# Hybrid decoder trunk, two layers on one core: another order of the attention stage around the projections

## The chip, the cores and the metric

One NeuronCore of a Trainium2 chip runs the whole program. The metric is the device time in microseconds (us) from start to end of one execution. TensorE (PE) multiplies, VectorE (DVE), ScalarE (ACT) and GpSimd (POOL) do the elementwise work, SyncE's queue (SP) issues the loads. Each engine works through its own list of instructions in order and waits on semaphores.

## The reference

256 tokens, width 1024, two layers. Per layer:

```python
h = rms_norm(x, attn_norm)
qa, ka, va, qd, kd, vd = split(h @ w_in)          # 6 groups of 512 columns, 8 heads of 64 each
out_a = rms_norm(causal_attention(rope(qa), rope(ka), va), moba_out_norm)
out_d = rms_norm(dilated_attention(rope(qd), rope(kd), vd), dil_out_norm)
x = x + concat(out_a, out_d) @ w_out
x = x + square(relu(rms_norm(x, mlp_norm) @ w_up)) @ w_down
```

and at the end `rms_norm(x, final_norm)`. With 256 tokens and blocks of 256 the block-sparse attention is plain causal attention. The dilated attention mixes three patterns of window and stride, each weighted by its softmax denominator; this is one softmax over the scores plus the logarithm of how many patterns hold the key.

## The kernel before

**Precision by splitting.** Every weight and every left operand exists as a high part (a cast) and a low part (the rest). ScalarE casts a unit of weights from `raw` to `w_hi` (`hi`, L447), VectorE subtracts it into `w_lo` (`lo`, L611), and PE makes three matmuls of 512 columns per product (`three`, L890 to L894). Weights come in chunks of two units; a ring holds four chunks, eight units. A load into a ring slot waits for the splits of the chunk that was there (`load`, L277), a cast waits until PE has used the unit that was in `w_hi` (`weights_used`, L445).

**Steps.** In a layer the input projection has 48 steps s, eight to each of the six groups, in the order dilated q, k, v, causal q, k, v (`GROUP_COLUMNS`). A step of `project_in` (L928) is one eighth of the depth for both token halves: six matmuls, three into the bank of each half; the groups take banks 0, 1 and 2, 3 in turn. Steps 48 to 55 are the output projection for the dilated heads. Then comes the projection for the causal heads, interleaved with steps 56 and 57, and the MLP.

**What hangs on the steps.** After the matmuls of step s, PE does in `attention(l, s)` (L988) what tables at L87 to L104 name for s:

- `ROPE_AT`, `V_AT` (s = 8, 16, ...): VectorE forms the rotation products of a finished q or k group, both token halves (`rope_products`, L656), and GpSimd sums them (`rope_sum`, L377); ScalarE copies a v group (L511).
- `QKT_AT`: PE turns rotated columns into `t_bank` in four transposes (L999), ScalarE copies them to `q_t` or `k_t` (L519). Before: steps 14, 15, 20, 21, 39, 41, 44, 47.
- `QK_PAIRS_AT`: PE makes the scores of a pair of heads, or of two pairs (`score_pair`, L964). Before: one pair at each of 23, 27, 31, 35, two at 46 and at 50.
- `QK_AT`: VectorE masks the scores of a head (L734, L737), ScalarE takes exponentials (L540). One step later, `NORM_AT`: VectorE normalises (`norm`, L635). Three steps later, `PT_AT`: PE turns the probabilities into the same `t_bank` (three transposes, L1008), ScalarE copies them (L526). Before: masks at 23, 25, ..., 37 and 46 to 53, so probability turnings at 26, 28, ..., 40 and 49 to 56.
- `PV_AT`: PE makes the products with v for one or two pairs of heads (L1024, L1027), ScalarE squares them and makes their high parts (L459, L462), VectorE the low parts (L626), GpSimd adds the squares (`add_squares`, L385).
- `STAT_D`: PE sums the squares of the dilated heads over columns (L1041), VectorE forms the mean (`o_mean`).

**The order on each engine is written out.** Within a step, ScalarE does v, the copy of rotated columns, the copy of turned probabilities, the product's squares and high parts, the exponentials, and last a cast (`HI_AT`) (L506 to L551). VectorE does mask, normalisation, rotation products, a split on odd steps only, low parts (L723 to L751). In `attention`, PE does the turning of rotated columns first, then that of probabilities, then products, scores, and the sum of squares. `t_bank` is one bank, so the turning of probabilities waits for every copy of rotated columns asked for up to this step:

```python
pe.wait_ge(p_copied, l * N_HEADS + h + 1)
pe.wait_ge(qk_copied, l * 8 + sum(x_ <= s for x_ in QKT_AT) + 1)
```

Of the kernel before, what the change touches and what calls it, by code (L numbers as in the profile page):

```python
# [37 lines left out]
ACT = mybir.ActivationFunctionType  # L38

P = 128  # L40
# [5 lines left out]
N_HEADS = D_MODEL // HEAD_DIM  # L46
# [9 lines left out]
TOK = SEQ // P  # L56
# [55 lines left out]
def hybrid_kernel(nc, x_d, w_in, w_out, w_up, w_down, final_g, gain_rows_d, ident_d, masks_d, rope_d,  # L112
                  out_d):
    ctx = ExitStack()
    with ctx:
# [3 lines left out]
        def sem(name):  # L119
            return ctx.enter_context(nc.semaphore(name))  # L120
# [72 lines left out]
        split_done = sem("split_done")  # L193
        weights_used = sem("weights_used")
        x_updated = sem("x_updated")
        x_mid = sem("x_mid")
# [47 lines left out]
        def used(l, u):  # L244

            return l * UNITS + u + (1 + UNITS_HELD)

        def turned_tile(x_or_m, k):
# [176 lines left out]
        def _(act):  # L425
# [46 lines left out]
            for l in range(DEPTH):  # L472
# [33 lines left out]
                for s in range(2 * ATT_UNITS):  # L506
                    if s in V_AT:
                        g = V_AT[s]
                        act.wait_ge(weights_used, used(l, 4 * g + 3))
                        act.wait_ge(rstd_done, l * STATS + ST_X + 1)  # L510
                        for t in range(TOK):  # L511
                            last = act.activation(v[:, V_GROUPS[g], t, :], banks[2 * (g % 2) + t][:, :],
                                                  ACT.Copy, scale=rstd[:, ST_X, t:t + 1])
                        last.then_inc(v_done, 1)
                    if s in QKT_AT:
# [88 lines left out]
        def _(dve):  # L604
# [51 lines left out]
            def rope_products(l, g, t):  # L656

                j = ROPE_GROUPS[g]
                dve.wait_ge(weights_used, used(l, 4 * g + 3))
# [4 lines left out]
                bank = banks[2 * (g % 2) + t]  # L664
# [28 lines left out]
            for l in range(DEPTH):  # L693
# [29 lines left out]
                for s in range(2 * ATT_UNITS):  # L723
                    u = s // 2 + LO_AHEAD
                    if s == STAT_D + 1:
                        o_mean(l, ST_D, stat_d)
                    if s in QK_AT:
# [4 lines left out]
                                 (exp_done, l * N_HEADS + h + 1))  # L732
                        bank = early_banks.get(h, s_banks[h % 2])
                        dve.tensor_tensor_reduce(out=scores[:, h % 2, 0:P], in0=bank[:, 0:P], in1=m[:, P:2 * P],  # L734
# [7 lines left out]
                    if s in ROPE_AT:  # L742
                        if ROPE_GROUPS[ROPE_AT[s]] == 0:
                            scale_rope(l)
                        for t in range(TOK):
                            rope_products(l, ROPE_AT[s], t)
                    if s % 2 == 1 and u < 2 * FIRST_UP + 1:
# [4 lines left out]
                    if s in X_AT:  # L752
# [5 lines left out]
                        add_to_x(acc_d[t][n], t, n, ST_D, x_d_added)  # L758
                o_mean(l, ST_A, stat_a)
                dve.wait_ge(rstd_done, l * STATS + ST_A + 1)  # L760
# [112 lines left out]
        def _(pe):  # L873
# [54 lines left out]
            def project_in(l, s):  # L928
                u = s // 2
                g, k = u // 4, u % 4 * 2 + s % 2  # L930
                c = u // 2
                cols = slice((k % 4) * BANK, (k % 4 + 1) * BANK)
                if l == 0 and s < 6:
                    first_project_in(k)
                    return
                if s == 1:
                    pe.wait_ge(first_lo_half, l)
                elif s % 2 == 0:
                    unit_ready(l, c, u % 2)
                if g == 0:  # L940
                    pe.wait_ge(turned_lo, l * TRS + TR_X + k + 1)
                if k == 0 and g in (2, 3, 5):

                    pe.wait_ge(rope_terms, l * 8 + 2 * ROPE_GROUPS[g - 2] + 2)
                if k == 0 and g == 1 and l == 0:
                    pe.wait_ge(gains_kept, 1)
                if k == 0 and g == 4:
                    pe.wait_ge(v_done, l * 2 + 1)
                for t in range(TOK):
                    tok = slice(t * P, (t + 1) * P)  # L950
                    last = three(banks[2 * (g % 2) + t][:, :], xt[:, k, 0, tok], xt[:, k, 1, tok],
                                 w_hi[:, c % RING, cols], w_lo[:, c % RING, cols], k == 0, k == KT - 1)
                    if t == TOK - 1 and s % 2 == 1:
                        last.then_inc(weights_used, 1)

# [8 lines left out]
            def score_pair(l, h):  # L964
                hh = h % SET_HEADS
                if hh % 4 == 0:

                    pe.wait_ge(qk_copied, l * 8 + 4 * (h // SET_HEADS) + hh // 4 + 4)
                if h == SET_HEADS:
                    pe.wait_ge(rope_terms, l * 8 + 8)  # L970
                elif h == SET_HEADS + 2:
                    pe.wait_ge(mean_done, l * STATS + ST_D + 1)
                elif h == SET_HEADS + 4:
                    pe.wait_ge(v_done, l * 2 + 2)
                elif h == SET_HEADS + 6:
# [3 lines left out]
                outs = [early_banks.get(h + e, s_banks[e]) for e in range(2)]  # L979
                rows = [slice(e * HEAD_DIM, (e + 1) * HEAD_DIM) for e in range(2)]  # L980
# [7 lines left out]
            def attention(l, s):  # L988
# [22 lines left out]
                if s in PV_AT:  # L1011
                    pairs = PV_AT[s]
                    st = pairs[0] // SET_PAIRS
                    pe.wait_ge(p_copied, l * N_HEADS + 2 * pairs[-1] + 3)
                    pe.wait_ge(v_done, l * 2 + st + 1)
# [76 lines left out]
            for l in range(DEPTH):  # L1092
# [56 lines left out]
                project_out(l, acc_a, 7, u0 + 3, 0, 0, False, True).then_inc(acc_a_done, 1)  # L1149
                sum_squares(l, 1, stat_a)  # L1150
                for t, n in ((1, 0), (0, 1)):
# [66 lines left out]
```

## Time and profile before

| what | value |
| --- | --- |
| median of 3 runs | 599.85 us (599.79 to 599.92) |
| the profiled execution | 599.85 us, span 598.1 us |
| busy PE, DVE, ACT, POOL | 589.3, 393.9, 316.8, 46.5 us |
| projection and attention, first layer | about 17 to 120 us of the span |
| the same in the second layer | about 303 to 412 us |
| chain that ended last | 98% PE |

Starts are counted from the start of the span. Matmuls are pipelined: the time that a matmul of a run adds is the distance of its start from the start before it, not its duration. The same holds for short instructions on VectorE and ScalarE.

### The profile page before, as it was taken

Reading aid. Unit: us, or ns where it says so; the run is one execution under the profiler, and the core shown is the slowest. Engines: PE = TensorE matmul, PEld = TensorE weight load, DVE = VectorE, ACT = ScalarE, POOL = GpSimd, SP = SyncE. Lnnn points to the kernel's source line nnn. Section 1 sums busy time; section 2 is a strip of 40 time slices with the busy share of each in tenths; the row PEclk is TensorE's granted clock in tenths of the full one; section 3 lists DMA queues with packets and bytes.
Section 4 is the critical chain, followed back from the end, with each engine's and each line's share of the span. In section 5 each row is a group of like instructions: output and inputs, shape, how many; then the busy total and the mean of one; then the engine's idle time right before and its main releaser. Section 6 shows DMA issues by size and latency. Waiting matters only on the chain.

```text
span 598.1 us, 8728 instructions
## 1 busy us (share of the span) xinstructions
PE 589.3 (99%) x3066; PEld 485.0 (81%) x3066; DVE 393.9 (66%) x655; ACT 316.8 (53%) x536; POOL 46.5 (8%) x51
## 2 busy tenths in 40 slices
PE   8999999999999999999999999999999999999995
PEld 5877777788888888888888777878888888888884
DVE  5866958687755755656388478677875755755634
ACT  5747749475535435344284567674654435435322
POOL 0220230110000000000004013001100000000001
PEclk9999999999999999999999999999999999999999
DMA  8954344248665464564266434431877465465301
GB/s 303 354 212 142 141 141 142 71 140 276 220 222 196 151 236 174 169 250 143 71 209 212 141 140 142 133 112 45 269 249 249 141 219 201 149 224 188 105 0 70
DMA packets 58842, 104.00 MB, mean 174 GB/s; under 512 B 1808, under 2 KB 35264, under 8 KB 58816
## 3 DMA queue, kind: packets, MB, share of 16 engines
q1 hardware_dynamic: 58320, 102.87, 50.7%
q10 hardware_dynamic: 496, 0.81, 0.4%
q8 instruction: 14, 0.23, 0.2%
q14 instruction: 12, 0.10, 0.1%
HBM read 102.62 MB, written 1.05 MB: 173 GB/s over the span
## 4 chain that ended last, share of the span: by engine, by line
PE 98%; DVE 1%; issue 0%; POOLq 0%; POOL 0%; ACT 0%; DVEq 0%; ACTq 0%
PE psum L1051 20%; PE psum L892 20%; PE psum L894 19%; PE psum L893 19%; PE psum L1054 10%; PE psum L1008 2%; PE psum L1024 1%; PE psum L899 1%; PE psum L999 1%; PE psum L985 1%; PE psum L983 1%; PE psum L882 1%; PE psum L1027 1%; PE psum L914 1%; PE psum L920 0%; PE psum L923 0%
## 5 line engine op out<-in xcount | busy, mean ns | idle before, releaser
L611 DVE TENSOR_TENSOR w_lo<-raw,w_hi 128x1024 fp32r<-128x1024 f32 x188 | 229.4, 1256 | 51.4 <-ACT w_hi L447 51.4
L447 ACT CAST w_hi<-raw 128x1024 fp32r<-128x1024 f32 x188 | 187.0, 1049 | 3.0 <-DMA raw<-in_w_in 3.0
L1051 PE MATMUL psum<-xt,w_hi 128*128 128x512 f32 x512 | 160.8, 395 | 0.0
L892 PE MATMUL psum<-w_hi,ot_hi 128*128 128x512 f32 x320 | 127.5, 398 | 0.0
L894 PE MATMUL psum<-w_hi,ot_lo 128*128 128x512 f32 x320 | 125.0, 391 | 0.0
L893 PE MATMUL psum<-w_lo,ot_hi 128*128 128x512 f32 x320 | 124.9, 390 | 0.0
L1054 PEld LDWEIGHTS psum<-xt,w_lo 128*128 128x128 f32 x512 | 96.2, 188 | 22.3
L1054 PE MATMUL psum<-xt,w_lo 128*128 128x256 f32 x512 | 100.8, 278 | 0.0
L1051 PEld LDWEIGHTS psum<-xt,w_hi 128*128 128x128 f32 x512 | 80.3, 189 | 2.3
L558 ACT COPY up_cross<-psum 128x512 f32<-128x512 f32 x32 | 18.8, 588 | 118.8 <-PE psum L1054 118.8
L892 PE MATMUL psum<-w_hi,xt 128*128 128x512 f32 x180 | 74.3, 413 | 0.0
L784 DVE TENSOR_TENSOR up_cross<-psum,up_cross 128x512 f32<-128x512 f32 x32 | 22.1, 692 | 74.0 <-ACT up_cross L558 74.0
L894 PE MATMUL psum<-w_hi,xt 128*128 128x512 f32 x180 | 70.7, 393 | 0.0
L894 PEld LDWEIGHTS psum<-w_hi,ot_lo 128*128 128x128 f32 x320 | 60.1, 188 | 12.9
L893 PE MATMUL psum<-w_lo,xt 128*128 128x512 f32 x180 | 70.4, 391 | 0.0
L892 PEld LDWEIGHTS psum<-w_hi,ot_hi 128*128 128x128 f32 x320 | 60.1, 188 | 12.6 <-issue 2.1
L893 PEld LDWEIGHTS psum<-w_lo,ot_hi 128*128 128x128 f32 x320 | 60.2, 188 | 10.4
L562 ACT CAST ot_hi<-up_sq 128x512 fp32r<-128x512 f32 x32 | 19.9, 622 | 56.3 <-DVE up_sq L787 56.3
L540 ACT ACTIVATE probs<-scores,row_bias 128x128 f32<-128x128 f32 x64 | 28.7, 451 | 25.2 <-DVE row_bias L737 25.2
L892 PEld LDWEIGHTS psum<-w_hi,xt 128*128 128x128 f32 x180 | 33.9, 188 | 9.2 <-issue 3.0
L894 PEld LDWEIGHTS psum<-w_hi,xt 128*128 128x128 f32 x180 | 33.8, 188 | 7.4
L893 PEld LDWEIGHTS psum<-w_lo,xt 128*128 128x128 f32 x180 | 34.0, 189 | 5.7
(85 smaller groups left out, 445.5 us busy)
## 6 DMA issues: line engine op xcount, KB each, us to landing
raw<-in_w_up SPq DMA_DIRECT2D x32, 1024.0 KB, 5.5
raw<-in_w_down SPq DMA_DIRECT2D x32, 1024.0 KB, 6.7
raw<-in_w_in SPq DMA_DIRECT2D x21, 1024.0 KB, 5.5
raw<-in_w_out SPq DMA_DIRECT2D x8, 1024.0 KB, 4.9
raw<-in_w_in SPq DMA_DIRECT2D x3, 512.0 KB, 7.8
raw<-in_w_in SPq DMA_DIRECT2D x4, 256.0 KB, 4.6
out<-x SPq DMA_DIRECT2D x3, 256.0 KB, 2.4
raw<-in_w_in ACTq DMA_DIRECT2D x2, 256.0 KB, 5.1
```

Source lines behind the costliest of these rows:

```text
L447: act.copy(w_hi[:, slot, part], raw[:, slot, part]).then_inc(hi_done, 1)
L540: last = act.activation(probs[:, h % 4, cols], scores[:, h % 2, cols], ACT.Exp, scale=-1.0, bias=row_bias[:, h % 2, t:t + 1], accum_out=ro ...
L558: act.copy(up_cross[:, :, :], up_banks[b][:, :, SEQ:2 * SEQ]).then_inc(cross_copied, 1)
L562: act.copy(h_hi[:, b, :, :], up_sq[:, :, :]).then_inc(h_hi_done, 1)
L611: dve.tensor_tensor(w_lo[:, slot, part], raw[:, slot, part], w_hi[:, slot, part].bitcast(F32), ALU.subtract).then_inc(split_done, 1)
L784: dve.tensor_tensor(up_cross[:, :, :], up_banks[b][:, :, 0:SEQ], up_cross[:, :, :], ALU.add)\
L892: pe.matmul(out, s_hi, m_hi, start=first, stop=False)
L893: pe.matmul(out, s_hi, m_lo, start=False, stop=False)
L894: return pe.matmul(out, s_lo, m_hi, start=False, stop=last)
L1008: last = pe.transpose(t_bank[:, n * P:(n + 1) * P], probs[:, h % 4, n * P:(n + 1) * P], ident[:, :])
L1051: pe.matmul(up_banks[b][:, f, :], w_hi[:, slot, cols[f]], xt[:, k, :, :].rearrange("p a b -> p (a b)"), start=k == 0, stop=False)
L1054: last = pe.matmul(up_banks[b][:, f, SEQ:2 * SEQ], w_lo[:, slot, cols[f]], xt[:, k, 0, :], start=False, stop=k == KT - 1)
```

## The change

Five things. The groups after the first go through banks 2 and 3 alone, and by token half: four steps for the first 128 tokens (all depths), then four for the others, each step six matmuls as before (group 0 keeps its old order, in a function `first_group` that is not shown); a new semaphore `half_done` tells that the first half is there, and rotation products and v copies are taken half by half. The dilated scores come four heads at a time, at steps 22 and 32, in banks 0, 1, 4 and 5. Masks of the dilated heads are at steps 22, 24, 26, 28 and 32, 34, 36, 38, so their probabilities are turned at 25, 27, 29, 31 and 35, 37, 39, 41. Turnings of rotated columns are at 14, 15, 19, 20, 37, 39, 43, 46; causal scores at 45 and 49; products at 32 (two pairs), 42, 52, 56. The sum of squares of the dilated heads goes from step 45 to 47 and from a score bank to the output bank. The order within a step, on every engine, stays.

```diff
-QK_AT = {23 + 2 * h if h < 8 else 38 + h: h for h in range(N_HEADS)}
+QK_AT = {22 + 2 * h if h < 4 else 24 + 2 * h if h < 8 else 37 + h: h for h in range(N_HEADS)}
 NORM_AT = {s + 1: h for s, h in QK_AT.items()}
 PT_AT = {s + 3: h for s, h in QK_AT.items()}
-PV_AT = {31: (0,), 35: (1,), 41: (2, 3), 53: (4, 5), 57: (6, 7)}
-QK_PAIRS_AT = {23: (0,), 27: (2,), 31: (4,), 35: (6,), 46: (8, 10), 50: (12, 14)}
-SQUARES_LATE = {58: (6, 7)}
+PV_AT = {32: (0, 1), 42: (2, 3), 52: (4, 5), 56: (6, 7)}
+QK_PAIRS_AT = {22: (0, 2), 32: (4, 6), 45: (8, 10), 49: (12, 14)}
+SQUARES_LATE = {57: (6, 7)}
 LAST_PAIR = {p: pairs[-1] for pairs in PV_AT.values() for p in pairs}
-QKT_AT = {14: 0, 15: 1, 20: 2, 21: 3, 39: 4, 41: 5, 44: 6, 47: 7}
-ROPE_AT = {8 * g + 8: g for g in ROPE_GROUPS}
-V_AT = {8 * g + 8: g for g in V_GROUPS}
+QKT_AT = {14: 0, 15: 1, 19: 2, 20: 3, 37: 4, 39: 5, 43: 6, 46: 7}
+ROPE_AT = {8: ((0, 0), (0, 1))} | {8 * g + 4 * t + 4: ((g, t),) for g in ROPE_GROUPS if g > 0 for t in range(TOK)}
+V_AT = {8 * g + 4 * t + 4: (g, t) for g in V_GROUPS for t in range(TOK)}
 TAIL = 56
-STAT_D = 45
+STAT_D = 47
...
-V_AT_LAST = max(V_AT)
-HI_AT = {s + int(s == V_AT_LAST): s // 2 + HI_AHEAD for s in range(0, 2 * ATT_UNITS, 2)}
+HI_AT = {s + int(s % 8 == 4 or s in V_AT): s // 2 + HI_AHEAD for s in range(0, 2 * ATT_UNITS, 2)}
...
-        early_banks = {8: banks[0], 9: banks[1], 12: banks[2], 13: banks[3]}
+        more_banks = {h: banks[h % 2] for h in (2, 3, 6, 7, 8, 9)} | {12: banks[2], 13: banks[3]}
...
-        stat_d, stat_a = s_banks[0][:, 3 * P:3 * P + TOK], o_bank[:, 0:TOK]
+        stat = o_bank[:, 0:TOK]
...
+        def group_bank(g, t):
+            return banks[2 * int(g > 0) + t]
...
             def project_in(l, s):
+                g = s // 8
+                if g == 0:
+                    first_group(l, s // 2, s)
+                    return
+                t, j = s % 8 // 4, s % 4
+                u = 4 * g + j
+                if t == 0:
+                    unit_ready(l, u // 2, u % 2)
...
+                if j == 0 and g - 1 in V_GROUPS:
+                    pe.wait_ge(v_done, l * 4 + t + 1)
+                elif j == 0 and g > 1:
+                    pe.wait_ge(rope_terms, l * 8 + 2 * ROPE_GROUPS[g - 1] + t + 1)
+                tok = slice(t * P, (t + 1) * P)
+                for k in (2 * j, 2 * j + 1):
+                    cols = slice((k % 4) * BANK, (k % 4 + 1) * BANK)
+                    last = three(group_bank(g, t)[:, :], xt[:, k, 0, tok], xt[:, k, 1, tok],
+                                 w_hi[:, u // 2 % RING, cols], w_lo[:, u // 2 % RING, cols], k == 0, k == KT - 1)
+                if t == 1:
+                    last.then_inc(weights_used, 1)
+                elif j == 3:
+                    last.then_inc(half_done, 1)
...
-                if h == SET_HEADS:
-                    pe.wait_ge(rope_terms, l * 8 + 8)
-                elif h == SET_HEADS + 2:
-                    pe.wait_ge(mean_done, l * STATS + ST_D + 1)
+                if h == 2:
+                    pe.wait_ge(rope_terms, l * 8 + 2)
                 elif h == SET_HEADS + 4:
-                    pe.wait_ge(v_done, l * 2 + 2)
+                    pe.wait_ge(v_done, l * 4 + 4)
                 elif h == SET_HEADS + 6:
                     pe.wait_ge(masked, l * N_HEADS + SET_HEADS + 4)
-                elif h >= 2:
-                    pe.wait_ge(masked, l * N_HEADS + h)
+                elif h >= 4:
+                    pe.wait_ge(masked, l * N_HEADS + h - 2)
...
+                    if pairs[0] == SET_PAIRS:
+                        pe.wait_ge(mean_done, l * STATS + ST_D + 1)
...
                 if s == STAT_D:
-                    pe.wait_ge(masked, l * N_HEADS + SET_HEADS)
-                    sum_squares(l, 0, stat_d)
+                    pe.wait_ge(o_split, l * PAIRS + SET_PAIRS)
+                    sum_squares(l, 0, stat)
```

## Rows read from the trace of the kernel before

**Rows 1.** The page, busy time and share of the span by engine.

```profile
PE 589.3 (99%) x3066; PEld 485.0 (81%) x3066; DVE 393.9 (66%) x655; ACT 316.8 (53%) x536; POOL 46.5 (8%) x51
```

**Rows 2.** PE's timeline, layer 0, steps 16 to 39: start, us, engine, line, op, count.

```profile
31.62 0.39 PE L893 MATMUL psum<-w_lo,xt 128*128 128x512 f32 x1
...
37.99 0.39 PE L894 MATMUL psum<-w_hi,xt 128*128 128x512 f32 x1
...
38.23 0.60 PE L999 MATMUL psum<-ident,roped 128*128 128x128 f32 x4
...
38.90 0.40 PE L893 MATMUL psum<-w_lo,xt 128*128 128x512 f32 x1
...
73.50 0.60 PE L999 MATMUL psum<-ident,roped 128*128 128x128 f32 x4
```

**Rows 3.** PE's timeline, layer 0, around three score steps.

```profile
43.02 0.39 PE L894 MATMUL psum<-w_hi,xt 128*128 128x512 f32 x1
...
43.33 0.49 PE L983 MATMUL psum<-k_t,q_t 64*128 64x128 f32 x4
...
44.53 0.39 PE L893 MATMUL psum<-w_lo,xt 128*128 128x512 f32 x1
...
57.16 0.40 PE L894 MATMUL psum<-w_hi,xt 128*128 128x512 f32 x1
...
59.48 0.39 PE L893 MATMUL psum<-w_lo,xt 128*128 128x512 f32 x1
...
86.66 0.40 PE L894 MATMUL psum<-w_hi,xt 128*128 128x512 f32 x1
...
88.84 0.40 PE L893 MATMUL psum<-w_lo,xt 128*128 128x512 f32 x1
```

**Rows 4.** PE's and VectorE's timelines, layer 0, first steps of the causal output projection.

```profile
113.14 0.40 PE L894 MATMUL psum<-w_hi,ot_lo 128*128 128x512 f32 x1
...
113.52 0.47 PE L892 MATMUL psum<-w_hi,ot_hi 128*128 128x512 f32 x1
...
112.89 0.88 DVE L626 SCALAR_TENSOR_TENSOR ot_lo<-psum,gains,ot_hi 128x256 fp32r<-128x256 f32 x2 [3.11 <-ACT ot_hi L462]
```

**Rows 5.** ScalarE's timeline, layer 0.

```profile
45.07 0.40 ACT L540 ACTIVATE probs<-scores,row_bias 128x128 f32<-128x128 f32 x1 [2.85 <-DVE row_bias L737]
...
45.97 1.24 ACT L512 ACTIVATE v<-psum,rstd 128x512 f32<-128x512 f32 x2
...
47.11 1.04 ACT L447 CAST w_hi<-raw 128x1024 fp32r<-128x1024 f32 x1
...
74.14 0.59 ACT L519 COPY q_t<-psum 128x512 f32<-128x512 f32 x1 [0.40 <-PE psum L999]
```

**Rows 6.** VectorE's timeline, layer 0.

```profile
31.45 0.68 DVE L671 TENSOR_TENSOR rope_a<-psum,rope_r 128x512 f32<-128x512 f32 x1
...
33.97 3.51 DVE L611 TENSOR_TENSOR w_lo<-raw,w_hi 128x1024 fp32r<-128x1024 f32 x2
...
44.40 0.29 DVE L734 CUSTOM_DVE_ANT_0 scores<-psum,masks 128x128 f32<-128x128 f32 x1 [5.78 <-issue]
...
44.96 1.22 DVE L611 TENSOR_TENSOR w_lo<-raw,w_hi 128x1024 fp32r<-128x1024 f32 x1
...
46.09 0.17 DVE L637 RECIPROCAL row_inv<-row_sum 128x2 f32<-128x2 f32 x1
...
46.76 0.29 DVE L734 CUSTOM_DVE_ANT_0 scores<-psum,masks 128x128 f32<-128x128 f32 x1
```

**Rows 7.** GpSimd: its timeline, and the tile `roped` (ns min/median/max).

```profile
34.13 2.27 POOL L382 TENSOR_TENSOR roped<-rope_a,rope_b 128x512 f32<-128x512 f32 x1
...
67.94 0.74 POOL L394 TENSOR_TENSOR o_sum<-o_sq 128x256 f32<-128x256 f32 x1 [1.87 <-ACT o_sq L459]
...
L382 POOL TENSOR_TENSOR roped<-rope_a,rope_b x16: 1284/1302/2274, 24.6 to 369.1; 128x512 f32<-128x512 f32 x16
```

**Rows 8.** Stretch behind PE's last matmul: busy us per engine, granted clock, DMA.

```profile
591.50:595.80 4.30, 0.00 (x0) 0.00 (x0) 2.98 (x5) 2.27 (x6) 1.14 (x2) 1.00 0.32 117
```

More of the change, by code:

```diff
@@ L194, in hybrid_kernel @@
         weights_used = sem("weights_used")
+        half_done = sem("half_done")
         x_updated = sem("x_updated")
@@ L246, in used, with half_group @@
             return l * UNITS + u + (1 + UNITS_HELD)
+        def group_bank(g, t):
+            return banks[2 * int(g > 0) + t]
+        def half_group(l, g):
+            return l * (GROUPS - 1) + g
         def turned_tile(x_or_m, k):
@@ L507, in _ @@
                     if s in V_AT:
-                        g = V_AT[s]
-                        act.wait_ge(weights_used, used(l, 4 * g + 3))
+                        g, t = V_AT[s]
+                        if t == 0:
+                            act.wait_ge(half_done, half_group(l, g))
+                        else:
+                            act.wait_ge(weights_used, used(l, 4 * g + 3))
                         act.wait_ge(rstd_done, l * STATS + ST_X + 1)
[L511 to L514, printed above, removed]
+                        act.activation(v[:, V_GROUPS[g], t, :], group_bank(g, t)[:, :], ACT.Copy,
+                                       scale=rstd[:, ST_X, t:t + 1]).then_inc(v_done, 1)
                     if s in QKT_AT:
@@ L658, in rope_products @@
                 j = ROPE_GROUPS[g]
-                dve.wait_ge(weights_used, used(l, 4 * g + 3))
+                if g > 0 and t == 0:
+                    dve.wait_ge(half_done, half_group(l, g))
+                else:
+                    dve.wait_ge(weights_used, used(l, 4 * g + 3))
                 dve.wait_ge(rope_scaled, l + 1)
@@ L663, in rope_products @@
                     dve.wait_ge(rope_done, l * 8 + 2 * (j - 1) + t + 1)
-                bank = banks[2 * (g % 2) + t]
+                bank = group_bank(g, t)
                 cos, sin, neg = (rope_r[:, t, n * HALF:(n + 1) * HALF] for n in range(3))
@@ L725, in _ @@
                     if s == STAT_D + 1:
-                        o_mean(l, ST_D, stat_d)
+                        o_mean(l, ST_D, stat)
                     if s in QK_AT:
@@ L732, in _ @@
                                  (exp_done, l * N_HEADS + h + 1))
-                        bank = early_banks.get(h, s_banks[h % 2])
+                        bank = more_banks.get(h, s_banks[h % 2])
                         dve.tensor_tensor_reduce(out=scores[:, h % 2, 0:P], in0=bank[:, 0:P], in1=m[:, P:2 * P],
@@ L742, in _ @@
                     if s in ROPE_AT:
-                        if ROPE_GROUPS[ROPE_AT[s]] == 0:
+                        if s == min(ROPE_AT):
                             scale_rope(l)
-                        for t in range(TOK):
-                            rope_products(l, ROPE_AT[s], t)
+                        for g, t in ROPE_AT[s]:
+                            rope_products(l, g, t)
                     if s % 2 == 1 and u < 2 * FIRST_UP + 1:
@@ L758, in _ @@
                         add_to_x(acc_d[t][n], t, n, ST_D, x_d_added)
-                o_mean(l, ST_A, stat_a)
+                o_mean(l, ST_A, stat)
                 dve.wait_ge(rstd_done, l * STATS + ST_A + 1)
@@ L928, in project_in @@
             def project_in(l, s):
[L929 to L933, printed above, removed]
+                g = s // 8
[4 more added lines that the diff above has]
+                u = 4 * g + j
+                if t == 0:
+                    unit_ready(l, u // 2, u % 2)
@@ new lines, in project_in @@
+                if j == 0 and g == 1 and l == 0:
+                    pe.wait_ge(gains_kept, 1)
+                if j == 0 and g - 1 in V_GROUPS:
[7 more added lines that the diff above has]
+                                 w_hi[:, u // 2 % RING, cols], w_lo[:, u // 2 % RING, cols], k == 0, k == KT - 1)
@@ L934, in project_in, with first_group @@
+                if t == 1:
+                    last.then_inc(weights_used, 1)
+                elif j == 3:
+                    last.then_inc(half_done, 1)
+            def first_group(l, u, k):
+                if l == 0 and k < 6:
                     first_project_in(k)
                     return
-                if s == 1:
+                cols = slice((k % 4) * BANK, (k % 4 + 1) * BANK)
+                if k == 1:
                     pe.wait_ge(first_lo_half, l)
-                elif s % 2 == 0:
-                    unit_ready(l, c, u % 2)
@@ L940, in project_in @@
[L940 to L948, printed above, removed]
+                elif k % 2 == 0:
+                    unit_ready(l, u // 2, u % 2)
+                pe.wait_ge(turned_lo, l * TRS + TR_X + k + 1)
@@ L949, in project_in @@
                 for t in range(TOK):
                     tok = slice(t * P, (t + 1) * P)
[L951 to L954, printed above, removed]
+                    last = three(group_bank(0, t)[:, :], xt[:, k, 0, tok], xt[:, k, 1, tok],
+                                 w_hi[:, u // 2 % RING, cols], w_lo[:, u // 2 % RING, cols], k == 0, k == KT - 1)
@@ L956, in project_out @@
+                if k % 2 == 1:
+                    last.then_inc(weights_used, 1)
             def project_out(l, acc, k, u, t, n, first, last):
@@ L968, in score_pair @@
                     pe.wait_ge(qk_copied, l * 8 + 4 * (h // SET_HEADS) + hh // 4 + 4)
-                if h == SET_HEADS:
-                    pe.wait_ge(rope_terms, l * 8 + 8)
-                elif h == SET_HEADS + 2:
-                    pe.wait_ge(mean_done, l * STATS + ST_D + 1)
+                if h == 2:
+                    pe.wait_ge(rope_terms, l * 8 + 2)
                 elif h == SET_HEADS + 4:
-                    pe.wait_ge(v_done, l * 2 + 2)
+                    pe.wait_ge(v_done, l * 4 + 4)
                 elif h == SET_HEADS + 6:
                     pe.wait_ge(masked, l * N_HEADS + SET_HEADS + 4)
-                elif h >= 2:
-                    pe.wait_ge(masked, l * N_HEADS + h)
-                outs = [early_banks.get(h + e, s_banks[e]) for e in range(2)]
+                elif h >= 4:
+                    pe.wait_ge(masked, l * N_HEADS + h - 2)
+                outs = [more_banks.get(h + e, s_banks[e]) for e in range(2)]
                 rows = [slice(e * HEAD_DIM, (e + 1) * HEAD_DIM) for e in range(2)]
@@ L1014, in attention @@
                     pe.wait_ge(p_copied, l * N_HEADS + 2 * pairs[-1] + 3)
-                    pe.wait_ge(v_done, l * 2 + st + 1)
+                    pe.wait_ge(v_done, l * 4 + 2 * st + 2)
                     if pairs[0] > 0:
                         pe.wait_ge(o_split, l * PAIRS + pairs[0])
+                    if pairs[0] == SET_PAIRS:
+                        pe.wait_ge(mean_done, l * STATS + ST_D + 1)
                     rows = [slice(e * HEAD_DIM, (e + 1) * HEAD_DIM) for e in range(2)]
@@ L1149, in _ @@
                 project_out(l, acc_a, 7, u0 + 3, 0, 0, False, True).then_inc(acc_a_done, 1)
-                sum_squares(l, 1, stat_a)
+                sum_squares(l, 1, stat)
                 for t, n in ((1, 0), (0, 1)):
```

## The prediction

> **What bounds the kernel now.** I read the page first: TensorE (PE) is busy 99% of the span [rows 1]. The list of waits names none for PE inside the two layers, and the chain that ended last is almost all PE's own instructions. So in the attention stage the time is PE's instructions, one after the other, plus what each change of kind costs. That is read from PE's timeline: from 31.62 to 37.99 there are 28 plain spacings, 0.227 us each, whether the bank changes (every third matmul) or not; a step of six takes 1.36 us. An interruption costs the distance from the last plain matmul before it to the second one after it, less 0.454: a lone turning of rotated columns 0.46 [rows 2], a lone pair of scores 1.06, a pair behind one product of values 1.87, four heads of scores together 1.73 [rows 3]. A turning of probabilities has three transposes instead of four: estimate 0.34.
>
> The other engines have slack there, but each works through an order written by hand, and this change shifts that order. So after PE's savings I walk VectorE, ScalarE and GpSimd.
>
> **What PE saves, per layer.** Two lone pairs become one four-head step: 2 x 1.06 - 1.73 = 0.39. Two steps of product and pair become one with two of each; no row shows it, so between 0.39 and twice that, taken at 0.5. In steps 37 and 39 the two kinds of turning now share a step: the restart of 0.09 falls away twice, 0.2. The wait of 0.15 at 113.14 [rows 4] goes, since the last product stands one step earlier with six more matmuls behind it. The sum of squares only changes place. Together 1.24, for both layers 2.5 us. Columns by token half: the same matmuls and weight loads, now 24 in a row into one bank; spacing doesn't depend on the bank in [rows 2], so 0, at most 0.3 either way.
>
> **Weights.** A group's four units are now wanted in its first four steps and released in its last four. Casts, splits and loads keep their count; a load on SP's queue waits for a split, so it comes later when VectorE does, and the ring of eight units covers that: 0, and one split (1.13) where the cover fails.
>
> **Other waits.** The mean at VectorE's step 48 stands before the mask of head 11, and products at 52 wait for it; its sum comes at 47, and the masks it delays are asked for two steps later: 0, and 0.2 if not.
>
> **What is added.** The decisive place is the second half of a dilated set. After the change, probability turnings stand at steps 35, 37, 39, 41, and QKT_AT puts the next turnings of rotated columns at 37 and 39. Both write the same bank. attention() does the rotated ones first, and the others then wait for qk_copied, whose count includes the copy just asked for. In the kernel before no step holds both. Behind the waiting turning on PE stand step 38 and all that follows, so a stall there is lost in full. The least price: 0.64 from turning to copy, 0.59 copy, 0.11 handoff, less 0.36 in which PE turns: 0.98 each [rows 2, 5].
>
> ScalarE, though, gets to that copy only behind what its order puts ahead: at step 36 the exponentials of head 6, which wait for VectorE's mask of head 6. And VectorE is slower per head than it was. Masks used to fall on odd steps: mask, split, then normalisation, so the exponential hid behind the split. Now masks fall on even steps and normalisation follows at once; VectorE stands through handoff, exponential and handoff. Prices: mask 0.56, split 1.13, normalisation 0.67, rotation products of one token half 1.26 [rows 6]; exponential 0.90, cast 1.04, handoffs 0.11 [rows 5]. A head costs VectorE 0.56 + 1.12 + 0.67 + 1.13 = 3.5 us; PE gives it two steps and a turning, 3.06.
>
> Walk from the first score matmul of step 32, time 0. The mask of head 4 starts at 1.07 (as 43.33 to 44.40) and ends at 1.63. Products of group 3's second half: 2.89. Two low parts of outputs (0.88) [rows 4]: 3.77. Normalisation: 4.44, and I add 0.37 for the rest of GpSimd's sum of that half, begun at 3.05, and 0.74 for its sum of squares behind it: 5.55. Split 6.68, mask of head 5 7.24, exponential and handoffs 8.37, normalisation 9.04, split 10.17, mask of head 6 10.73, its exponentials 11.74, the copy 12.33, PE goes on at 12.44. Unhindered PE would be there at 9.13: second matmul of step 33 at 1.85 (88.84 less 86.99, where 86.99 is 86.66 and 0.33), 29 spacings, one turning 0.34, and 0.36 for the rotated turning. **Stall 3.3 us.** From there to step 39's second turning: 3.42, so 15.86. VectorE meanwhile: products 11.99, normalisation of head 6 with GpSimd's sum 13.94, split 15.07, mask of head 7 15.63, exponentials 16.64, ScalarE's cast of step 38 17.68, copy 18.27, handoff 18.38. **Stall 2.5 us.** In the first half of the set the same lag, with products and a GpSimd sum between mask and normalisation of head 3, brings that normalisation to 15.3 after the scores of step 22; PE wants it at 14.9: 0.5. Behind 41 there are free steps, and the second set overlaps as it did. Per layer 6.3, for two 12.6.
>
> In layer 0 only, the turning at step 19 waits too. VectorE is packed from the rotation of group 0 on; the second rotation half ended at 33.97 and its sum at 36.40 [rows 6, 7], the turning came at 38.23 [rows 2]. Now it is due at 36.86, and an additional GpSimd sum falls among the splits, which it holds by 1.1: the sum ends at 37.5. With the handoff 0.8. In layer 1 VectorE was idle before that rotation: 0.
>
> The GpSimd terms rest on a meeting that rows show for splits: its sum takes 1.28 alone and 2.27 beside a split, and two splits take 3.51 instead of 2.3 [rows 6, 7]. No row shows it beside a normalisation, so between 0 and 1.28 each; I take the whole, since a normalisation, like a split, works from SBUF to SBUF. By the Trainium skill, "SBUF — State Buffer", section "Who interferes with whom", GpSimd and a VectorE instruction with two SBUF inputs, or a tensor_scalar in a two-port mode, lock each other out for a whole instruction. By that rule the sum is the one below; without it for normalisations it would be some 4 us less. No row here shows the second half of the rule.
>
> **Sum:** 12.6 + 0.8 - 2.5 = 10.9 us over the profiled execution. Its own time is 599.85 (span 598.1 and 1.7 around it), which is also the median of the three runs. 599.85 + 10.9 = 610.8.
>
> **The rivals.**
> 1. GpSimd doesn't hold normalisations. Then step 37 stalls 2.2, step 39 2.0, step 31 not at all: 8.4 + 0.8 - 2.5, 606.6 us. Chance 0.23.
> 2. Only the copy counts, because VectorE is not late: 4 x 0.98 - 2.5, 601.3 us. The head's 3.5 against 3.06 speaks against it. Chance 0.09.
> 3. Faster: the second turning in steps 37 and 39 starts without PE standing, and only the savings are left: 597.4 us. It decides from below 0.6 us per doubled step. PE's never waiting today speaks for it, the wait's count and the 0.98 against it. Chance 0.08. With stalls just about that, no change: 599.9, chance 0.03.
> 4. The pauses drop PE's clock. With PE idle for 4.30 us at the kernel's end the granted clock was still 1.00 [rows 8], and no pause here is longer than 3.3. If it fell to its lower level (1.2 of 2.4 GHz) after each of four pauses and some 3 us of matmuls took double, 6 to 8 us more: 618. Chance 0.05. The Trainium skill, "TensorE: Matmul & The Clock Gate", section "Why this matters for your kernels", warns that a long idle gap between bursts puts the clock back; on that page's word this rival would have more weight than the row gives it.
>
> The forecast itself, 608.5 to 613, has 0.52.
>
> **How the numbers follow.** The forecast and rival 1 hold 0.75; the range goes down to rival 2, and up by what the walk may be short of (a late cast, a second handoff): 601.2 to 613.2. A measurement of this kernel can tell about 0.2%, 1.2 us, from no change. Slower: forecast, rivals 1 and 4, and most of 2: 0.87. Same 0.05, faster 0.08. Within the slower cases the likeliest one's own range is 608.5 to 613.
>
> **What the profile after would show.** PE busy falls to about 97%. Two idle times per layer stand between a turning of rotated columns and one of probabilities, 3 and 2.5 us long, released by ScalarE's copy; ScalarE's copy is preceded by an exponential that waited for a mask; VectorE waits for exponentials ahead of each reciprocal of heads 0 to 7. Score steps of the dilated set: one of 1.73 and one near 3.2 per layer. No idle time at the output projection's third weight. I am wrong if the copies are released by the turning itself (rival 2), if no mask runs late, or if PE shows no idle time in steps 37 and 39 at all.

## The result, and the profile after

The changed kernel takes 609.25 us, the median of six runs (609.12 to 610.87); the kernel before took 599.88 beside it (599.78 to 600.14, six runs). The ratio is 1.0162, 95% interval 1.0149 to 1.0175: slower, as forecast, by 9.4 us where 10.9 were forecast. The profiled execution took 609.24, its span is 607.5 against 598.1.

The page of the changed kernel: the span, busy time by engine, and the chain that ended last (compare [rows 1]).

```profile
span 607.5 us, 8731 instructions
...
PE 591.2 (97%) x3066; PEld 487.2 (80%) x3066; DVE 399.7 (66%) x655; ACT 317.3 (52%) x536; POOL 49.8 (8%) x51
...
PE 37%; DVE 2%; issue 1%; ACT 0%; POOLq 0%; POOL 0%; ACTq 0%; DVEq 0%
```

PE has as many matmuls as before, and its share falls from 99 to 97%. The 37% of the last line can't be set beside the 98% of before: here the chain was followed back only to 354.30, in the second layer. The waits of PE say where the time went: line waited at, what ended the wait, total, times, longest.

```profile
PE psum L1034 <- ACT q_t L528: 5.6, 4, 2.0
PE psum L894 <- DVE squares L695: 1.7, 1, 1.7
PE psum L926 <- ACT xt L461: 0.9, 2, 0.5
PE psum L1025 <- ACT probs_t L535: 0.7, 2, 0.4
PE psum L1025 <- POOL roped L390: 0.4, 1, 0.4
```

L1034 is the turning of probabilities, L528 the copy of rotated columns: four waits, at steps 37 and 39 of both layers. L926 stands ahead of the attention stage of layer 0 (0.3 us once in the kernel before). The last line is step 19 of layer 0. Here are these places in PE's timeline of layer 0 (start, us; the last bracket is idle time before). The rows run from the last plain matmul before step 37's turnings to the product behind step 39's.

```profile
70.00 0.39 PE L906 MATMUL psum<-w_hi,xt 128*128 128x512 f32 x1
70.75 0.63 PE L1025 MATMUL psum<-ident,roped 128*128 128x128 f32 x4 [0.36 <-ACT probs_t L535]
73.41 0.88 PE L1034 MATMUL psum<-ident,probs 128*128 128x128 f32 x3 [2.02 <-ACT q_t L528]
73.93 0.78 PE L904 MATMUL psum<-w_hi,xt 128*128 128x512 f32 x1
74.50 0.63 PE L905 MATMUL psum<-w_lo,xt 128*128 128x512 f32 x1
74.93 0.63 PE L906 MATMUL psum<-w_hi,xt 128*128 128x512 f32 x1
...
76.52 0.40 PE L904 MATMUL psum<-w_hi,xt 128*128 128x512 f32 x1
...
77.89 0.60 PE L1025 MATMUL psum<-ident,roped 128*128 128x128 f32 x4
79.26 0.52 PE L1034 MATMUL psum<-ident,probs 128*128 128x128 f32 x3 [0.77 <-ACT q_t L528]
...
79.85 0.39 PE L905 MATMUL psum<-w_lo,xt 128*128 128x512 f32 x1
```

Two things are to be seen. First the pause: with no wait the second turning would have come 0.227 + 0.36 = 0.59 behind 70.00, and it came 3.41 behind it, so 2.82 us late. Part of this stands ahead of the first turning, which also had to wait, for the copy of head 4's probabilities. Second, the matmuls after the pause: 74.50 to 74.93 is 0.43, almost twice the plain 0.227. The stretches show why: busy us of PE, its weight loads, VectorE, ScalarE and GpSimd (with counts), then the granted clock, DMA share and GB/s.

```profile
71.20:73.30 2.10, 0.18 (x2) 0.00 (x0) 2.06 (x10) 1.45 (x5) 0.18 (x1) 0.92 0.33 49
73.00:76.30 3.30, 2.90 (x9) 2.44 (x10) 3.27 (x8) 1.68 (x3) 1.27 (x1) 0.50 0.78 310
76.40:79.00 2.60, 2.09 (x12) 1.52 (x10) 1.51 (x6) 2.41 (x6) 0.00 (x0) 1.00 0.00 0
...
369.95:373.30 3.35, 3.35 (x11) 2.68 (x10) 2.73 (x7) 2.00 (x5) 0.70 (x1) 0.50 0.57 230
```

The granted clock is 1.00 until late in the pause, 0.50 (1.2 GHz) from about 73.0 to about 76.3, and 1.00 again. In layer 1 it falls at about 369.9, 0.2 us after the second turning has begun (369.67). From the turning at 73.41 to the seventh plain matmul (76.52) are 3.11 us; in layer 1's step 39 the same instructions take 1.74 at full clock. The slow clock costs 1.37 in layer 0 and 1.57 in layer 1, where it holds over two matmuls more.

The chain that ended last goes through the same place in layer 1 (start, us, what). It runs from a split on VectorE over the mask of head 6, its exponentials and the copy to PE's second turning of step 37.

```profile
366.27 1.22 DVE w_lo L620
367.49 0.20 DVE scores L746
...
368.38 0.68 ACT probs L549 x3
369.06 0.48 ACT q_t L528
...
369.67 0.65 PE psum L1034 x3
```

Why the copy came late is in ScalarE's and VectorE's timelines, layer 0.

```profile
71.81 0.40 ACT L549 ACTIVATE probs<-scores,row_bias 128x128 f32<-128x128 f32 x1 [1.20 <-DVE row_bias L749]
...
72.70 0.56 ACT L528 COPY q_t<-psum 128x512 f32<-128x512 f32 x1
...
76.45 0.40 ACT L549 ACTIVATE probs<-scores,row_bias 128x128 f32<-128x128 f32 x1 [0.71 <-DVE row_bias L749]
...
77.35 1.04 ACT L455 CAST w_hi<-raw 128x1024 fp32r<-128x1024 f32 x1
78.53 0.59 ACT L528 COPY q_t<-psum 128x512 f32<-128x512 f32 x1
```

```profile
65.27 1.32 DVE L650 TENSOR_SCALAR probs<-probs,row_inv 128x128 f32<-128x128 f32 x2
66.51 1.21 DVE L620 TENSOR_TENSOR w_lo<-raw,w_hi 128x1024 fp32r<-128x1024 f32 x1
...
71.14 0.28 DVE L746 CUSTOM_DVE_ANT_0 scores<-psum,masks 128x128 f32<-128x128 f32 x1
...
73.14 1.59 DVE L650 TENSOR_SCALAR probs<-probs,row_inv 128x128 f32<-128x128 f32 x2
74.65 1.21 DVE L620 TENSOR_TENSOR w_lo<-raw,w_hi 128x1024 fp32r<-128x1024 f32 x1
75.79 0.27 DVE L746 CUSTOM_DVE_ANT_0 scores<-psum,masks 128x128 f32<-128x128 f32 x1
...
77.67 0.55 DVE L650 TENSOR_SCALAR probs<-probs,row_inv 128x128 f32<-128x128 f32 x2
```

The mask of head 6 starts at 71.14, the exponentials wait for it until 71.81, and the copy for the exponentials until 72.70, though its turning was finished over a microsecond earlier (70.75 and 0.63). At step 39 it is otherwise: the copy at 78.53 comes 0.64 behind its turning (77.89), which is the plain distance of [rows 2, 5]. There ScalarE had begun its cast at 77.35 and was nearly through it, so it was not late; only the copy itself counts.

GpSimd's sum and a normalisation meet twice per layer: 73.14 against 73.11 here, and 65.27 against 64.46.

```profile
64.46 1.29 POOL L390 TENSOR_TENSOR roped<-rope_a,rope_b 128x512 f32<-128x512 f32 x1 [6.76 <-DVE rope_b L687]
65.71 0.74 POOL L402 TENSOR_TENSOR o_sum<-o_sq 128x256 f32<-128x256 f32 x1
73.11 1.27 POOL L390 TENSOR_TENSOR roped<-rope_a,rope_b 128x512 f32<-128x512 f32 x1 [6.67 <-DVE rope_b L687]
```

A normalisation takes 0.55 alone (77.67), 1.59 where it starts with the sum, and 1.32 where it starts in its middle and the sum of squares (65.71) follows. The hold on normalisations, which no row of before showed, is there: 1.04 and 0.77.

### The profile page after: what moved, and what is told of

It is laid out like the page before. It is cut to its first block and busy times, and to the rows that moved or that the text cites. A ratio compares the mean times of both kernels' runs of the same rounds, so it can differ in the third digit from the quotient of the medians.

```text
span 607.5 us, 8731 instructions
## 1 busy us (share of the span) xinstructions
PE 591.2 (97%) x3066; PEld 487.2 (80%) x3066; DVE 399.7 (66%) x655; ACT 317.3 (52%) x536; POOL 49.8 (8%) x51
## 5 line engine op out<-in xcount | busy, mean ns | idle before, releaser
L904 PEld LDWEIGHTS psum<-w_hi,xt 128*128 128x128 f32 x180 | 34.6, 192 | 8.4 <-issue 2.3
L906 PEld LDWEIGHTS psum<-w_hi,xt 128*128 128x128 f32 x180 | 34.5, 192 | 7.7
```

Of the source, the lines that this page charges most:

```text
L904: pe.matmul(out, s_hi, m_hi, start=first, stop=False)
L906: return pe.matmul(out, s_lo, m_hi, start=False, stop=last)
```

## The experiments

Eight kernels were run. A cost of a step is counted as in the prediction, by distances of plain matmuls.

**Turnings apart.** The changed kernel, with the turnings of rotated columns one step earlier, where no probabilities are turned.

```diff
-QKT_AT = {14: 0, 15: 1, 19: 2, 20: 3, 37: 4, 39: 5, 43: 6, 46: 7}
+QKT_AT = {14: 0, 15: 1, 19: 2, 20: 3, 36: 4, 38: 5, 43: 6, 46: 7}
```

> The changed kernel with the third and fourth-last turnings of rotated columns at steps 36 and 38 instead of 37 and 39, so that no step holds both kinds of turning. Theory (the shared steps make PE wait for ScalarE's copy, which stands behind an exponential that waits for a late mask): the two long waits per layer go, and with them the fall of the clock. What is left is the lag of VectorE and ScalarE itself: some 0.9 us before step 38's turning and 0.6 before step 41's, 0.3 at step 31, and 0.65 in layer 0 at step 19: 601 to 602.5 us. Rival A (only the copy itself costs, 1 us a step, the rest of the loss lies elsewhere, in the order by token half): 605 us. Rival B (VectorE is so late that the place of the turning hardly matters): above 607.

Measured 602.53 us (602.41 to 602.60), ratio 1.0043 [1.0027, 1.0060]. So 6.7 of the 9.4 us hung on the shared steps, with the slow clock behind them. The time is at the upper edge of what was expected, but what was left was not where it was expected: steps 38 and 41 cost nothing, but the turning at 36 waits in both layers.

```profile
PE psum L1025 <- ACT probs_t L535: 3.4, 2, 1.7
...
70.50 0.63 PE L1025 MATMUL psum<-ident,roped 128*128 128x128 f32 x4 [1.70 <-ACT probs_t L535]
```

It waits for the copy of head 4's turned probabilities, and that copy stands on ScalarE behind head 5's exponentials and a cast. The granted clock stays at 1.00 here in both layers, through a pause of 1.7 us (1.87 lost).

**The shared step alone.** The kernel before, with its turnings at 39 and 41 moved onto the probability turnings at 38 and 40.

```diff
-QKT_AT = {14: 0, 15: 1, 20: 2, 21: 3, 39: 4, 41: 5, 44: 6, 47: 7}
+QKT_AT = {14: 0, 15: 1, 20: 2, 21: 3, 38: 4, 40: 5, 44: 6, 47: 7}
```

> The kernel before with one edit: two turnings of rotated columns go from steps 39 and 41 to 38 and 40, where probabilities are turned as well. Masks stay on odd steps, so VectorE is in time. Theory: each shared step costs the copy alone, 0.98 us, less 0.1 for the restart that is saved: 4 x 0.9 = 3.5 us more, 603.4, and the clock stays at 1.00, since a pause is about 1 us. Rival (the late masks are all of it, a shared step by itself costs nothing): 599.7.

Measured 603.78 (603.60 to 603.85), ratio 1.0065 [1.0048, 1.0082]: 3.9 us for four shared steps. PE's timeline, one of the four, and the copy:

```profile
71.70 0.60 PE L999 MATMUL psum<-ident,roped 128*128 128x128 f32 x4
...
73.07 0.52 PE L1008 MATMUL psum<-ident,probs 128*128 128x128 f32 x3 [0.77 <-ACT q_t L519]
...
72.34 0.59 ACT L519 COPY q_t<-psum 128x512 f32<-128x512 f32 x1
```

Here nothing on the other engines is late, and the copy starts 0.64 behind the turning: the doubled step costs 1.74 instead of 0.45 + 0.345 for the two turnings apart, so 0.94 more. That is the least price, forecast at 0.98 less 0.1 for the merged restart. In this schedule a step with both turnings isn't free.

**The split ahead of the normalisation.** The changed kernel with VectorE's order in odd steps up to 41 changed to mask, split, normalisation, so that the exponentials hide again.

```diff
+                    if s % 2 == 1 and s <= 42:
+                        lo(l, u // 2, u // 2 % RING, u % 2)
...
-                    if s % 2 == 1 and u < 2 * FIRST_UP + 1:
+                    if s % 2 == 1 and u < 2 * FIRST_UP + 1 and s > 42:
```

> The changed kernel, turnings at 37 and 39 as they are; only VectorE's order is edited: on odd steps up to 41 the split comes before the normalisation. Theory (late masks lengthen the wait of step 37 over the copy's own 1 us, and that long pause is what drops the clock): mask of head 6 comes about 0.5 us earlier, PE is held 0.7 us at step 35 instead, so step 37 stands for 1 to 2 us and the clock stays at 1.00; time between 605 and 607.5. Rival (the order on VectorE doesn't matter, the copy behind the exponential does): 609 and the fall of the clock as before.

Measured 605.04 (604.83 to 605.31), ratio 1.0086 [1.0070, 1.0101]: 4.2 us less than the changed kernel and just inside what was expected. Step 31 doesn't wait any more, step 37 costs 1.75 (the least price), and the clock stays at 1.00. But step 35 now costs 1.06 instead of 0.34, and step 39 2.64 instead of 1.73. Counted from the first score matmul of step 32, the copy at step 39 starts 1.5 us earlier than in the changed kernel (15.60, it was 17.11). PE gets there 2.4 us earlier (14.05, it was 16.47), and so waits longer. VectorE's lag decides a good part, though not all; the walk's place for it was right.

**Both together.** The two edits above in one kernel.

> As the run before it, and VectorE also does its split before the normalisation on the odd steps up to 41, so that the exponential can pass behind a split. Theory (VectorE standing through each exponential is what makes masks late): the waits at steps 38 and 41 go, but the normalisation of head 4 now stands behind a split and a GpSimd sum and costs about 1.2 us at step 35: 600 to 601 us. Rival (the lag comes from GpSimd's port and the rotation products, not from the exponentials): no better than the run before it, 601.5 or more.

Measured 602.11 (601.93 to 602.18), ratio 1.0037 [1.0022, 1.0051]. By its time this goes with the rival, though it is 0.4 less than with the turnings apart: the two savings, 6.7 and 4.2, don't add up. PE's waits show what is left, normalisation of head 4 behind the split and GpSimd's sum (step 35), and the copy of head 4 behind it (step 36).

```profile
PE psum L1027 <- ACT probs_t L535: 2.1, 2, 1.0
...
PE psum L1036 <- DVE probs L650: 1.0, 2, 0.5
```

**Something for PE to do in the pause.** The changed kernel with eight bf16 matmuls between the two turnings of step 37. They write a score bank that is free then, and nobody reads them.

```diff
+                    if s == 37:
+                        pe.wait_ge(masked, l * N_HEADS + 5)
+                        for _ in range(8):
+                            pe.matmul(s_banks[0][:, :], squares[:, 1, 0:P], squares[:, 1, 0:BANK],
+                                      start=True, stop=True)
```

> The changed kernel with eight bf16 matmuls of 512 columns, whose result nobody reads, put on PE between the two turnings of step 37 in each layer; they take 1.7 of the 2.2 us for which PE stood there. Theory (the clock fell because of that pause, but the slow stretch of 3.4 us mostly covers the next wait, at step 39, which is set by ScalarE): granted clock 1.00 throughout both layers, the wait of step 39 grows from 1.0 to about 2 us, and the time falls by only 0.5 to 1.5 us, to about 608.3. Rival A (the fall of the clock is lost in full): 2.6 us less, 606.7. Rival B (the clock falls all the same): no change or slower.

Measured 609.07 (four executions: 608.27, 608.20, 609.87, 609.87), ratio 1.0157 [1.0140, 1.0174]. PE's timeline of the profiled one, 608.27, layer 0, and a stretch of it:

```profile
70.93 1.89 PE L1031 MATMUL psum<-squares 128*128 128x512 bf16 x8
...
73.12 0.52 PE L1039 MATMUL psum<-ident,probs 128*128 128x128 f32 x3 [0.29 <-ACT q_t L528]
...
78.72 0.52 PE L1039 MATMUL psum<-ident,probs 128*128 128x128 f32 x3 [1.87 <-ACT q_t L528]
```

```profile
71.00:80.00 9.00, 6.83 (x35) 4.72 (x34) 7.88 (x22) 6.01 (x15) 1.28 (x1) 1.00 0.37 118
```

The clock stays at 1.00 in both layers, the second turning of step 37 comes as late as before, and step 37 costs 3.5 with no slow matmuls behind it. But step 39 now costs 2.84 instead of 1.73. So the slow clock cost the changed kernel 1.4 and 1.6 us and gave 1.1 back each time, because a PE that is late to step 39 waits less there: 0.7 us net. The attention stages are 0.3 and 0.45 us shorter than in the changed kernel. The rest of the 1.0 us between the two spans (606.5 and 607.5) lies ahead of them, where PE waits less at L926.

By the medians the filler gained only 0.2 us (609.07 against 609.25), less than was expected, since two of its executions are 1.6 us longer than the others. Their mean granted clock was 0.994 and 0.995, against 0.997 and 0.996. These have no trace. The clock may have fallen once in them, perhaps at the new pause of 1.87; that isn't shown.

**Turnings placed where nothing waits.** The changed kernel with the turnings at free or later steps, and the split ahead of the normalisation in seven steps only.

```diff
-QKT_AT = {14: 0, 15: 1, 19: 2, 20: 3, 37: 4, 39: 5, 43: 6, 46: 7}
+QKT_AT = {14: 0, 15: 1, 20: 2, 21: 3, 34: 4, 42: 5, 43: 6, 46: 7}
+SPLIT_FIRST = (23, 25, 27, 29, 31, 35, 39)
```

> The changed kernel with three things edited by what the runs so far showed. Turnings of rotated columns at 14, 15, 20, 21, 34, 42, 43, 46: at 34 and 42 no probabilities are turned, the bank is free and ScalarE has no exponential or cast ahead of the copy; at 20 GpSimd's sum is done. VectorE's split comes before the normalisation at steps 23 to 31, 35 and 39, not at 33 and 37. Theory: all the savings of the change (2.6 us) and no wait for a copy; left is a wait of some 0.5 us per layer for the normalisations of heads 6 and 7: 597.5 to 598.8, faster than the kernel before. Rival (the order by token half costs something on PE or in the weights' ring that the waits hid): 599.5 or more.

Measured 599.16 (599.07 to 599.52, eleven runs) beside 599.93, ratio 0.9989 [0.9980, 0.9998]: a little faster, but 0.4 over what was expected, between theory and rival. One wait is left per layer, 0.8 us at step 41, for the normalisation of head 7. PE's and VectorE's timelines:

```profile
76.64 0.52 PE L1037 MATMUL psum<-ident,probs 128*128 128x128 f32 x3 [0.64 <-DVE probs L651]
```

```profile
72.44 1.21 DVE L621 TENSOR_TENSOR w_lo<-raw,w_hi 128x1024 fp32r<-128x1024 f32 x1
73.58 0.28 DVE L747 CUSTOM_DVE_ANT_0 scores<-psum,masks 128x128 f32<-128x128 f32 x1
```

A split stands ahead of head 7's mask, and another behind it ahead of the normalisation. Whether they are the cause, or the order by token half, the last run tells.

**Scores by two instead of four.** The kernel just described, with the dilated scores a pair at a time.

```diff
-QK_PAIRS_AT = {22: (0, 2), 32: (4, 6), 45: (8, 10), 49: (12, 14)}
+QK_PAIRS_AT = {22: (0,), 24: (2,), 32: (4,), 34: (6,), 45: (8, 10), 49: (12, 14)}
```

> The run before it with one edit: the dilated scores again two heads at a time, at steps 22, 24, 32 and 34. Theory (four at a time saves one lone interruption and one merged one per layer, as the rows of before price them): 0.39 at the first, about 0.4 to 0.5 at the second, so 0.8 per layer and 1.6 to 1.9 us in all over the run before it. Rival (score steps are hidden by the waits of PE for VectorE): no difference.

Measured 600.58 (600.40 to 600.77), ratio 1.0010 [1.0001, 1.0019], 1.4 us more than with four, where 1.6 to 1.9 were expected. In the first set two lone pairs cost 1.06 each against 1.72 together, 0.40 less for the merge, forecast 0.39. In the second set the two steps cost 1.06 more, and the wait of 0.8 at step 41 is gone. So 2 x (0.40 + 1.06 - 0.82) = 1.3. Of the 1.06 some 0.65 is a wait for GpSimd's sum at step 34 (an estimate: the step costs 2.21, a turning at step 34 alone 0.51 and a lone pair 1.06). The gain of four at a time, 0.4, is measured in the first set; in the second it is what is left beside this wait.

**Splits out of the way.** The placed kernel with VectorE's splits of steps 37 and 39 moved to 39 and 40, ahead of the normalisation and of the rotation products there.

```diff
-SPLIT_FIRST = (23, 25, 27, 29, 31, 35, 39)
+SPLIT_FIRST = (23, 25, 27, 29, 31, 35, 39, 40)
+LO_AT = {s: s // 2 + LO_AHEAD for s in range(1, 2 * ATT_UNITS, 2) if s != 37} | {39: 22, 40: 23}
...
-                    u = s // 2 + LO_AHEAD
+                    u = LO_AT.get(s, 2 * FIRST_UP + 1)
...
-                    if s % 2 == 1 and u < 2 * FIRST_UP + 1 and s not in SPLIT_FIRST:
+                    if u < 2 * FIRST_UP + 1 and s not in SPLIT_FIRST:
```

> The placed version (599.16 us) with one more edit on VectorE: its splits of steps 37 and 39 move to 39 and 40, ahead of the normalisation and of the rotation products there. Theory (the 0.8 us that PE stands at step 41 of each layer is VectorE's late mask of head 7, behind a split that nobody needs yet): the mask comes 1.1 us earlier, the wait goes, 597.4 to 597.9 us, all of the 2.6 us that the change saves. Rival (the split is wanted by PE at step 42, or GpSimd's sum takes the place that came free): 598.5 or more.

Measured 597.43 us (597.37 to 597.75), ratio 0.9960 [0.9947, 0.9974] against the kernel before, as expected. It is faster than the kernel before and the changed one. Its page, and all that its list of waits holds for PE:

```profile
PE 587.0 (99%) x3066; PEld 485.4 (81%) x3066; DVE 399.0 (67%) x655; ACT 317.0 (53%) x536; POOL 51.7 (9%) x51
...
PE 97%; DMA 1%; DVE 0%; issue 0%; POOLq 0%; POOL 0%; ACTq 0%; DVEq 0%
```

```profile
PE psum L898 <- DVE squares L697: 1.7, 1, 1.7
```

Span 595.7, 2.4 less than before, with no wait of PE left but one of 1.7 us at the kernel's start, which is the same in every kernel here. So the order by token half was not what cost the placed kernel its wait. These 2.4 us are what the change saves when no turnings share a step; the change as made had covered them with stalls.

## Why the prediction was right, and where it was off

The direction, the mechanism and the place were right. That the sum, 10.9 us against 9.4, came out so close was partly luck, since two of its terms missed by 2.9 in opposite directions. Both layers together:

| term | forecast, us | measured, us |
| --- | --- | --- |
| savings, with the merged turnings | -2.5 | -2.8 (2.4 in the kernel with the splits moved, and 4 x 0.1 for the turnings that share a step) |
| step 19, layer 0 | 0.8 | 0.65 |
| step 31 | 1.0 | 2 x 0.30 |
| step 37, PE standing | 6.6 | 2.82 + 2.80 |
| slow clock behind step 37 | 0 | 1.37 + 1.57 |
| step 39 | 5.0 | 2 x 1.03 |
| outside the attention stages | 0 | 0.3 |
| sum | 10.9 | 9.4 |

**Savings.** Scores and products per layer went from 5.86 to 4.90: 0.96, forecast 0.89. Columns by token half cost nothing: 0.227 in runs of 24 into one bank. The wait of [rows 4] is gone. Two turnings in one step, without their wait, cost 0.70 (0.36 and 0.34) instead of 0.80. These steps of the prediction hold.

**Step 37.** The order of events was as walked: late mask, exponentials, copy. The mask of head 6 started at 9.72 from the first score matmul of step 32 (61.42), walked 10.17. All of these 0.45 us arose at one point, the normalisation of head 4, which ended at 5.09 instead of 5.55: low parts 0.1 earlier, and GpSimd held it by 0.77, not by the 0.37 + 0.74 that I added. PE went on at 11.99 instead of 12.44.

**Step 39, the step that failed.** "To step 39's second turning: 3.42, so 15.86" took PE at its full clock, against a copy walked to 18.27. By the trace PE's first turning there stood at 16.47, 0.97 later than walked in spite of its earlier start, since the matmuls between ran at half clock. And ScalarE was through its cast at about 17.0 (77.35 and 1.04) instead of 17.68, because VectorE had gained another 0.25 (mask of head 7 at 14.37, walked 15.07). With both shifts the copy followed its turning at the plain distance, at 17.11, and the stall shrank to the least price: the step costs 1.73, 1.03 over the 0.70 of a shared step without a wait. The kernel with the shared step alone has the same 1.73 to 1.74 (0.94 over two separate turnings). With the filler, where the clock stays up, the stall at 39 is 2.14: then the walk's 2.5 is nearly met.

**Rival 4** had the mechanism that I did not include: its clock fell at step 37 in both layers. Its price was far off: two falls instead of four, 1.4 and 1.6 us each, most of it returned at step 39; the filler puts the net at 0.7 us. My reason against it, 4.30 idle us at the kernel's end at clock 1.00 [rows 8], came from a stretch that ended just before the fall. The trace of the kernel before, right behind it:

```profile
595.80:598.10 2.30, 0.00 (x0) 0.00 (x0) 0.00 (x0) 0.00 (x0) 0.00 (x0) 0.51 0.63 237
```

So the idle PE did lose the clock there, about 4.4 us behind the end of its last matmul; in the placed kernel it did so after 1.9 us. The Trainium skill's warning against long idle gaps ("TensorE: Matmul & The Clock Gate", section "Why this matters for your kernels") should have had the more weight; the trace agrees in that the clock fell at 73 and 370 us, with PE standing 2.02 us.

**Rival 1** fell: GpSimd does hold a normalisation, 1.59 against 0.55. By the rule of "SBUF — State Buffer", section "Who interferes with whom", of the Trainium skill, this was to be expected, and the trace agrees (1.59 and 1.32 beside the sum). **Rival 2** was half right: "only the copy" is what happened at step 39, and at step 37 once VectorE's order was changed. **Rival 3** is ruled out by the kernel with the shared step alone, 0.94 each, over its limit of 0.6; the 597.4 that it named was reached, though, by the kernel that removes the doubled steps.

**Not settled:** what exactly lets the clock fall. The length of one pause alone doesn't tell. Inside the layers a pause of 2.02 us came with it in both layers; pauses of 1.7 (turnings apart) and 1.87 (step 39 with the filler, in the profiled execution) did not. At the end of the program, where all ten profiled executions do the same, the fall came between 1.9 us (the placed kernel) and 4.9 us (the kernel with the splits moved) behind the last matmul. What PE did ahead of the pauses differs too: ahead of the 2.02 it had stood for 0.36 and done only four transposes. I made no run that varies this alone. Four scores at a time were not tried alone on the kernel before, since its projection uses the banks that they need.

## What to carry to other kernels

When steps are moved in a schedule written out by hand, look first for two uses of one buffer that now fall into one step: with an engine's copy between them this cost 0.94 us each time here even with no other engine late, and much more where the copy stands in a queue behind work that is itself late. A merge that saves 0.4 us can be lost many times over if the queues that feed it don't move with it: here the same change went from 9.4 us slower to 2.4 us faster once four turnings stood at other steps, two splits came later, and VectorE did its split earlier within eight steps. And in a walk along a stalled engine, what makes it late to the second wait shortens that wait, as long as the second one's releaser isn't delayed as well: stalls in a row don't simply add.

## What the hardware showed that I had not expected

PE's granted clock fell to half around a pause of 2.02 us (counted between the two turnings), in both layers, and stood at 1.00 again after some 3 us in which PE worked. Eight matmuls put in the pause of step 37 kept it up in the profiled execution. At the kernel's end it falls in every profiled execution, but at moments from 1.9 to 4.9 us behind the last matmul. So a stretch that shows 1.00 in an idle time proves little about the next one, and the mean granted clock of an execution moves by up to 0.004 with this alone (an estimate: 4.8 us at half clock in the 597.5 of the placed kernel). And a normalisation, one input and a column of factors, is held by GpSimd for almost the whole of its 1.27 us instruction when both start together (1.59 instead of 0.55).
